# A scaling moved from ScalarE to VectorE, and the odd layer's copy put ahead of the next norm, in a hybrid decoder step

## What is computed

```python
ALPHA = (2 * DEPTH) ** 0.25        # DEPTH = 2
x = _layernorm(ALPHA * x + mixer(x), ln_g[layer, 0], ln_b[layer, 0])
x = _layernorm(ALPHA * x + _moe(x, w_router, ...), ln_g[layer, 1], ln_b[layer, 1])

def _moe(x, ...):                  # 16 experts in 4 groups: best group, then the top 2 in it
    scores = sigmoid(h @ w_router)
    ...
    for e in range(16):
        he = silu(h @ w_gate[e]) * (h @ w_up[e])
        y = y + gates[:, e:e + 1] * (he @ w_down[e])
```

## Time and profile before

| | us |
|---|---|
| median of 3 runs | 1346.32 (1345.76 to 1350.44) |
| time of the profiled execution | 1346.32 |
| its span, first to last instruction | 1344.5 |
| TensorE busy | 1107.2 (82%) |
| VectorE busy | 518.3 (39%) |
| ScalarE busy | 303.4 (23%) |
| POOL busy | 140.8 (10%) |

### The profile page before, as it was taken

How to read it: one execution, slowest core, us unless ns; L and a number is a source line. 1 busy time by engine, 2 the same in 40 slices (tenths; PEclk the granted TensorE clock), 3 DMA queues, 4 the chain that set the end, 5 groups by cost and what they waited for, 6 DMA issues and landing times.

```text
span 1344.5 us, 18666 instructions
## 1 busy us (share of the span) xinstructions
PE 1107.2 (82%) x7162; PEld 674.7 (50%) x7162; DVE 518.3 (39%) x1332; ACT 303.4 (23%) x691; POOL 140.8 (10%) x177
## 2 busy tenths in 40 slices
PE   0999996599999089999899989976599839999920
PEld 0477453344444057777788865533355424444400
DVE  1183236111111454497556545634223521111145
ACT  0111114111111122332343322533211221111111
POOL 0001001100000300000211114132100020000030
PEclk9999998699999589999999978978889959999965
DMA  9229206999992712123333204133410499999451
GB/s 392 54 102 315 36 1 238 355 341 369 373 355 96 250 63 94 64 95 105 119 101 106 88 2 183 65 141 142 195 63 0 157 336 370 369 365 363 151 187 62
DMA packets 62753, 244.16 MB, mean 182 GB/s; under 512 B 7840, under 2 KB 28384, under 8 KB 45120
## 3 DMA queue, kind: packets, MB, share of 16 engines
q1 hardware_dynamic: 35856, 146.07, 30.2%
q0 software_dynamic: 16992, 77.66, 15.8%
q10 hardware_dynamic: 9808, 19.14, 3.9%
HBM read 203.55 MB, written 56.06 MB: 193 GB/s over the span
## 4 chain that ended last, share of the span: by engine, by line
PE 75%; DVE 8%; issue 8%; DMA 6%; ACT 1%; POOL 1%; POOLq 0%; DVEq 0%; ACTq 0%
PE bank L1199 16%; PE bank L1140 9%; PE bank L1219 8%; PE bank L1345 8%; PE bank L1269 5%; PE bank L1442 4%; PE bank L1287 3%; DMA xT<-in_xT_dram 2%; PE bank L1189 2%; PE bank L1319 2%; DVE acc L2243 2%; DVE stat L2044 1%; PE bank L1696 1%; PE bank L1151 1%; PE bank L1128 1%
## 5 line engine op out<-in xcount | busy, mean ns | idle before, releaser
L1140 PE MATMUL bank<-ring,cat 128*128 128x512 f32 (+1 forms) x320 | 140.7, 594 | 1.8 <-ACT cat L1832 1.3
L1199 PE MATMUL bank<-ring,work 128*128 128x512 f32 x256 | 113.8, 596 | 0.0
L1345 PE MATMUL bank<-xT,ring 128*128 128x288 f32 x448 | 110.9, 407 | 0.0
L2223 DVE TENSOR_TENSOR work<-work,bank 128x256 f32<-128x256 f32 x32 | 13.5, 422 | 218.7 <-ACT work L1811 218.7
L1345 PEld LDWEIGHTS bank<-xT,ring 128*128 128x128 f32 x448 | 84.6, 190 | 24.1 <-issue 1.5
L1140 PEld LDWEIGHTS bank<-ring,cat 128*128 128x128 f32 (+1 forms) x320 | 56.1, 179 | 74.3 <-issue 73.6
L1199 PEld LDWEIGHTS bank<-ring,work 128*128 128x128 f32 x256 | 48.0, 192 | 54.1 <-issue 54.1
L1269 PE MATMUL bank<-xT,ring 128*128 128x288 f32 x256 | 63.1, 407 | 0.0
L1287 PE MATMUL bank<-ring,xT 128*128 128x512 f32 (+1 forms) x80 | 36.5, 617 | 30.9 <-DMA xT<-in_xT_dram 30.9
L1189 PE MATMUL bank<-const,work 128*128 128x128 f32 x256 | 36.4, 292 | 28.2 <-DMA work<-xrows 28.2
L1811 ACT ACTIVATE work<-bank 128x256 f32<-128x256 f32 x32 | 12.3, 385 | 207.4 <-PE bank L1199 207.4
(11 more groups left out here) (429 smaller groups left out, 1938.0 us busy)
## 6 DMA issues: line engine op xcount, KB each, us to landing
ring<-in_stream_dram SPq DMA_DIRECT2D x71, 1024.0 KB, 8.5
cat<-in_stream_dram SPq DMA_DIRECT2D x16, 1024.0 KB, 8.9
work<-xrows ACTq DMA_DIRECT2D x32, 512.0 KB, 5.9
xT<-in_stream_dram SPq DMA_DIRECT2D x16, 1024.0 KB, 9.0
work<-in_stream_dram SPq DMA_DIRECT2D x16, 1024.0 KB, 10.9
yrows<-work POOLq DMA_DIRECT2D x32, 512.0 KB, 9.2
by_batch<-in_pages_dram SPq DMA_DIRECT2D x128, 128.0 KB, 2.4
xrows<-work POOLq DMA_DIRECT2D x1, 8192.0 KB, 27.4
```

The lines of the kernel that those rows point to most:

```text
L1140: i = pe.matmul(bank(n)[0:ROWS[tile], :], cat[:, k, tok(tile)], slot(w[k // 4], 4, 512)[:, k % 4, :], start=(k == 0), stop=(k == KC - 1))
L1199: i = pe.matmul(bank(n), xgT[:, e % 2, k, :], sparse_slot(layer, 3 * e + k // 4, 4, 512)[:, k % 4, :], start=(k == 0), stop=(k == KC - 1))
L1345: i = pe.matmul(bank(n + s)[:, 0:nn], slot(w, KC, 256)[:, k, P * (m % 2):P * (m % 2) + P], xT[:, k, a:a + nn], start=(k == 0), stop=(k == ...
```

## The change

Two edits. The five scalings of acc leave ScalarE and become five VectorE instructions behind `assign(layer, 1)`, in both layers; the semaphore `acc_scaled` goes. In the odd layer's ScalarE program `copy_xT` of a tile is put ahead of `norm` of the next tile.

```diff
@@ -547,7 +547,6 @@
-        acc_scaled = sem("acc_scaled")
@@ -1775,10 +1774,6 @@
                 router_scores(layer, 1)
-                act.wait_ge(ln_done, (2 * layer + 1) * NT)
-                for tile in range(NT):
-                    r = ROWS[tile]
-                    act.activation(acc[0:r, tile, :], x[0:r, tile, :], ACT.Copy, scale=ALPHA).then_inc(acc_scaled, 1)
                 flag = is_crowded(act, layer)
@@ -1854,9 +1849,9 @@
             def odd():
                 norm(1, 0)
                 for tile in range(NT):
+                    copy_xT(f"xT{tile}", tile)
                     if tile + 1 < NT:
                         norm(1, tile + 1)
-                    copy_xT(f"xT{tile}", tile)
                     if tile > 0:
                         latent_rows(tile - 1)
                 latent_rows(NT - 1)
@@ -2184,7 +2179,10 @@
                 route(layer, 1)
                 assign(layer, 1)
-                dve.wait_ge(acc_scaled, NT * (layer + 1))
+                for tile in range(NT):
+                    r = ROWS[tile]
+                    i = dve.tensor_scalar(acc[0:r, tile, :], x[0:r, tile, :], ALPHA, None, ALU.mult)
+                step(i)
                 flag = is_crowded(dve, layer)
```

## The result

The changed kernel takes 1357.22 us (median of 5 runs, 1354.62 to 1358.41), the kernel before 1349.73 us in 5 runs (1345.76 to 1350.44; three of them are those shown ahead of the prediction, and the two later ones took 1349.73 and 1350.39). The ratio is 1.0062, with a 95% interval of 1.0042 to 1.0084: slower by 8.4 us (1349.73 x 0.0062), with 5.7 to 11.3 as the interval. The profiled execution took 1357.87 us, its span 1356.1. The prediction drew a line at half a per cent and gave 0.59 to a time over it; since the interval begins at 0.42%, the runs show a loss but don't settle on which side of that line it lies.

A forecast was written before the change was run, and what follows sets the result against it. The prediction took TensorE to be three quarters of the chain, with both edits where the chain leaves it or it waits. It summed 1346.3 + 5.0 (odd front) + 3.0 (port hold) = 1354.3 us, range 1350.3 to 1358.0.

The forecast's parts named there:

- the middle case of the port hold: At POOL's last four scatters, VectorE's scalings hold some issues briefly: 1.5 us a layer, 3.0 us for two layers.
- VectorE shuts POOL out until its five instructions end: Rival at POOL's late scatters: full hold through all five scalings, 6.2 us for two layers, 1357.5 us in all; chance 0.18.
- upper bound of 3.1 us: Hold per layer at POOL's late scatters: the scalings' 3.4 us less the 0.3 us before POOL's first issue.
- It passes to the end in full: From the last scatter on, landing, row loads and expert work are chained, so all 3.0 us of hold reach the end.
- part 1: Hand-over from routing to experts, both layers: scaling by ALPHA moved to VectorE, forecast to cost 3.0 us.
- Part 2: Odd layer's front: ScalarE's copy ahead of the next tile's norm, forecast to cost 5.0 us, bounds 4.0 to 5.5.
- Forecast turns: Odd front, from one tile's transposes to the next's: 9.91 us at the low clock, 9.03 at the high.
- the lower bound: Odd front: a shift of 4.0 us, with steps overlapping by a tenth of a us or two.
- Undisturbed scatters: Rival at POOL's late scatters: VectorE's scalings don't hold them and cost nothing, 1351.3 us in all; chance 0.20.
- Freed norm 3: Rival in the odd front: norm 3 comes sooner and T3 starts earlier, 1.28 us gained, 1345.0 us; chance 0.03.
- Swallowed shift: Rival in the prepare stage behind the odd front: part of the 5.0 us vanishes; with half, 1351.8 us; chance 0.06.
- Falling clock: Rival in the odd front: TensorE's clock falls in the new gaps, 1.4 us more, 1355.7 us; chance 0.05.

The follow-up runs named there:

- the seven unheld kernels: The kernel before and six follow-up kernels whose late scatters were not held up; middle time from crowded to first expert transposes 11.91 us in layer 0, 12.71 in layer 1.
- part 1 alone: Against the kernel before, only the five scalings moved to VectorE, with the odd layer's order as before: 1350.74 us, ratio 1.0016.
- part 2 alone: Against the kernel before, only the copy put ahead of the next tile's norm in the odd layer, scalings still on ScalarE: 1355.83 us, ratio 1.0048.
- one order of the odd front: Against the kernel before, odd layer's front on TensorE reordered to T0 L0 T1 L1 T2 T3 L2 T4 L3 L4, ScalarE's order following: 1348.12 us, ratio 1.0000.
- 0.93 us in the next: Against the kernel before, odd layer's front on TensorE reordered to T0 L0 T1 L1 T2 L2 T3 T4 L3 L4, ScalarE's order following: 1344.38 us, ratio 0.9974.

## Why the prediction was right or wrong

**The step that failed is the middle case of the port hold**, "nearer to the rows in which POOL slips in than to the full hold", at 1.5 us a layer. The first issue took 3.57 us in place of 0.96 in both layers: 2.6 us. That is the rival "VectorE shuts POOL out until its five instructions end", and the sign named for it, a first issue of 3 us or more, came. Its upper bound of 3.1 us was 0.5 too high, since five scalings took 3.08 us in place of 3.4, and the issue, which takes 0.96 us anyway, needs only 0.84 us more once the hold ends. (In the 3.4 us the step of 0.52 ns a column stands in no row; the first scaling took 0.67 us and each further one 0.60 in place of 0.78 and 0.66.)

The reading behind the middle case was wrong in kind. I took the earlier trace rows to show that POOL slips in between VectorE instructions. Only the overlap at 1296.60 shows that, and there a semaphore wait stands between the two; I wrote this down as the rival's argument and gave it 0.18. The overlap at 877.43 has no such wait: `L2637` issues its two tensor_scalars one behind the other, and POOL came under the second, so the end of the instruction and the end of the run are the same moment. That issue ended at 878.62, 0.85 us behind the run's end at 877.77, which is what the full hold gives too. "None of the overlaps shows a hold beyond the running instruction" is true, but the one at 877.43 could not have shown it, and the other had the wait. With waits put in, the holds were 0.21, 0.19 and 0.17 us; without them, three runs of different length and two kinds of instruction held the issue to their end. The forecast also spread the loss over several issues; in fact one issue bore all of it, and the other three ran free in the time after 243.63.

**"It passes to the end in full" was only nearly right.** TensorE started later by 2.42 and 1.88 us, not 2 x 2.6, and against the middle of the seven unheld kernels by 2.42 and 1.41. With part 1 alone the whole kernel lost 2.2 us (0.9 to 3.4). So the forecast's 3.0 us for the part lies inside the measurement, while its mechanism was not what happened: a hold 1.7 times as long and a loss of some of it behind the hold came out near the same sum. That is luck.

**Part 2 was right step by step.** Forecast turns 9.91, 9.91, 9.03; measured 9.82, 9.82, 8.96. Forecast shift 5.0 us; measured 4.74 with both parts and 4.75 with part 2 alone. The loop through the square root is shown by the kernel that moved only that instruction ahead of the copy and lost nothing. The 0.1 us a turn is the square root's start under the end of the copy (471.44 against 471.55), an overlap that the lower bound allowed for. From T3 on TensorE ran without a hole into the next stage, so the shift was not swallowed. The chain's row for L3 and L4 is 11.52 us again and the prepare stage follows at once, so the later parameter load was covered, as said.

**The rivals.** Undisturbed scatters: false, by the 3.57 us. Freed norm 3: false, T3 came 4.75 us later. Swallowed shift: false. Falling clock: false in its place, as the window from 490 to 509 has a full grant; L1 and L2 took 5.75 us. It held through the 2.28 us of idle time ahead of T3. A fall did come elsewhere, at the 96 matmuls of 654.95, and cost 0.87 us in the profiled execution.

**The sum.** Forecast +8.0 us; measured +8.4 by the ratio. The absolute time is 2.9 us over the forecast because its base, 1346.3, was low: 5 runs of the kernel before have a median of 1349.7. For the same reason the rival's 1357.5 us is close to the measured 1357.2 by chance; its rise of 11.2 us is more than the measured 8.4. The sum came out well since part 2, 5.0 of its 8.0 us, was right and part 1 lost less in time than it was held.

**The page of the Trainium skill.** The rule of "SBUF — State Buffer", section "Who interferes with whom", spoke for the upper bound and was right in that: whoever comes second is fully blocked. The runs go further, since POOL was held here through a whole back-to-back run and not through one instruction. The section also says that an instruction with two SBUF inputs contends with GpSimd's reads; the trace agrees, with an issue of 6.24 us. Whether it is the reading of the indices or the writing of descriptors that is held, no run here tells apart.

## What to carry to other kernels

When work is moved to VectorE at a place where POOL issues transfers, count it as one block as long as its back-to-back run, unless there are waits inside; VectorE's idle time in the profile says nothing about that. Before relying on overlaps found in a trace, look whether the instructions there stood under the same conditions (here: waits between them), and whether the overlap could have shown the rival at all. In an order written out by hand across several engines, find the one short instruction that another engine waits for, and keep it ahead of everything that waits itself. Before reading a stretch's change from two traces, look how much it differs between traces of kernels that left it alone.

## What was not expected of the hardware

- A gapless run of VectorE instructions held one POOL issue to its end: 1.77, 3.57 and 6.24 us for runs of 1.27, 3.08 and 5.74 us.
- Between VectorE's last instruction ahead of the read of a flag with its branch and the first one behind it passed 6.38 us (5.74 in layer 1) that no busy row shows. Here they are free only as long as they run under something else.
- In layer 1 the last scatter landed in 3.96 to 3.99 us in the three kernels that issued it 2.6 us later or more, in 4.45 and 4.18 us in the two with holds of 0.57 and 0.8 us, and in 4.79 to 5.79 us in the seven that held no issue; why was not tried.
- In one order of the odd front, with 1.21 and 1.99 us of idle time on either side of T3, the clock fell under L2 (7.52 us); behind 0.93 us in the next it did not (5.83 us), nor in the changed kernel behind 2.28 us ahead of T3. So the length of one idle stretch alone doesn't tell, and the gain of a shorter path can be lost again.
